# Feed-forward of a two-layer encoder step: the second hidden chunk with seven products in place of eight

## What is computed

```
def conv_ffn(x, conv_prev, w_up, conv_w, conv_b, w_down):
    u = x @ w_up
    ...
    c = conv_b
    for j in range(CONV_W):
        c = c + ue[:, j:j + T] * conv_w[j]
    a, b = jnp.split(c, 2, axis=-1)
    y = (jax.nn.silu(a) * b) @ w_down
    return y, ue[:, -(CONV_W - 1):]
```

## Time and profile before

| | us |
|---|---|
| median of 3 runs | 2957.55 (2957.21 to 2961.5) |
| the profiled execution, its own time | 2962.58 |
| its span, first to last instruction | 2960.7 |
| TensorE busy (95% of the span) | 2817.0 |
| VectorE busy (67%) | 1970.3 |
| ScalarE busy (37%) | 1098.0 |
| GpSimd busy (36%) | 1065.4 |

### The profile page before, as it was taken

The page is one execution under the profiler, slowest core; times in us unless marked ns, Lnnn a source line. Parts: engine busy times, 40 slices in busy tenths (PEclk is TensorE's granted clock), DMA queues, the critical chain, the costliest instruction groups (busy, mean ns, idle before and its releaser), DMA issues. The chain is left out here.

```text
span 2960.7 us, 47459 instructions
## 1 busy us (share of the span) xinstructions
PE 2817.0 (95%) x16927; PEld 2494.1 (84%) x16927; DVE 1970.3 (67%) x3414; ACT 1098.0 (37%) x2110; POOL 1065.4 (36%) x852
## 2 busy tenths in 40 slices
PE   8899799998999999999998898998999999999997
PEld 7455578886899999997887798997899999998886
DVE  3466654566578888888656464455468888888556
ACT  5334542333344333432113464334354333432112
POOL 1244421111236666662225101111136666662224
PEclk9999899999999999999999899999999999999999
DMA  3100350113212122124222111113212122124222
GB/s 116 51 8 13 121 186 22 37 40 111 86 65 81 66 74 81 66 91 175 91 91 94 54 37 42 30 45 114 83 67 81 66 74 81 66 91 175 91 91 102
DMA packets 90614, 233.61 MB, mean 79 GB/s; under 512 B 21514, under 2 KB 35995, under 8 KB 89428
## 3 DMA queue, kind: packets, MB, share of 16 engines
q1 hardware_dynamic: 90484, 231.85, 22.2%
HBM read 181.97 MB, written 50.50 MB: 79 GB/s over the span
## 5 line engine op out<-in xcount | busy, mean ns | idle before, releaser
L135 PE MATMUL psum<-xT_hi,tk_w 128*128 128x320 f32 (+1 forms) x1536 | 453.6, 295 | 2.8 <-ACT tk_u L2531 2.8
L137 PE MATMUL psum<-xT_hi,tk_w 128*128 128x320 f32 (+1 forms) x1536 | 453.7, 295 | 0.0
L136 PE MATMUL psum<-xT_lo,tk_w 128*128 128x320 f32 (+1 forms) x1536 | 452.5, 295 | 0.0
L2267 POOL TENSOR_TENSOR tk_w<-tk_sums,tk_w 128x512 fp32r<-128x512 f32 x160 | 306.9, 1937 | 170.3 <-ACT tk_w L2551 170.3
L135 PEld LDWEIGHTS psum<-xT_hi,tk_w 128*128 128x128 f32 x1536 | 289.4, 188 | 3.1 <-issue 3.1
L136 PEld LDWEIGHTS psum<-xT_lo,tk_w 128*128 128x128 f32 x1536 | 289.6, 189 | 0.0
L137 PEld LDWEIGHTS psum<-xT_hi,tk_w 128*128 128x128 f32 x1536 | 288.9, 188 | 0.0
L135 PE MATMUL psum<-tk_t,tk_w 128*128 128x256 f32 x960 | 284.4, 296 | 2.9 <-POOL tk_w L2267 2.9
L137 PE MATMUL psum<-tk_t,tk_w 128*128 128x256 f32 x960 | 284.5, 296 | 0.0
L136 PE MATMUL psum<-tk_t,tk_w 128*128 128x256 f32 x960 | 283.8, 296 | 0.0
L2949 DVE TENSOR_TENSOR x_or_mix<-x_or_mix,psum 128x512 f32<-128x512 f32 x288 | 195.3, 686 | 130.0 <-PE psum L137 129.3
(11 more groups left out here) (454 smaller groups left out, 7071.8 us busy)
## 6 DMA issues: line engine op xcount, KB each, us to landing
tk_wraw<-in_w_up SPq DMA_DIRECT2D x88, 512.0 KB, 4.2
ates_between_projections<-tk_g SPq DMA_DIRECT2D x44, 576.0 KB, 2.8
tk_graw<-ates_between_projections SPq DMA_DIRECT2D x44, 576.0 KB, 6.3
tk_draw<-in_w_down SPq DMA_DIRECT2D x44, 512.0 KB, 5.4
x_between_sublayers<-x_or_mix SPq DMA_DIRECT2D x18, 512.0 KB, 2.6
tk_resid<-x_between_sublayers SPq DMA_DIRECT2D x18, 512.0 KB, 7.9
s_ckv<-in_c_ckv SPq DMA_DIRECT2D x8, 1024.0 KB, 6.5
retw_raw<-in_w_ret SPq DMA_DIRECT2D x32, 256.0 KB, 3.3
```

Source lines behind the costliest of these rows:

```text
L135: nc.tensor.matmul(out, a[0], b[0], start=first, stop=False)
L136: nc.tensor.matmul(out, a[0], b[1], start=False, stop=False)
L137: return nc.tensor.matmul(out, a[1], b[0], start=False, stop=last)
L2267: nc.gpsimd.tensor_tensor(W7[:, i, 1], src, W7[:, i, 0].bitcast(F), ALU.subtract).then_inc(wl, 1)
```

## The change

Chunk 1 takes seven products too: `STD` goes from 2 to 1, the loops over seven-product chunks run one turn more (LOOP from 18 to 19), and `ORDER1`, `BANK1` and chunk 1's standard steps go. Now chunk 1 is the chunk in which T1 to T4 are used first. On DVE the four sums of weights stand ahead of the sums of x; the low halves of T2 and T3 stand right behind the sums of x, with chunk 0's convolution cut in two around T4's, and chunk 0's gate, which used to stand ahead of all of them, goes behind T1's. `t2_front` moves to the place of the gate's output, since `tk_sums` now holds its own place at that time. Of the raw weights chunk 2's go into `wraw` once chunk 1's A22 is split.

```
-    t2 = (m.at(tag + "t2_front", 90112, [P, 3, 576]), m.at(tag + "t2_end", 78848, [P, 1, 576]))
+    t2 = (m.at(tag + "t2_front", 9376, [P, 3, 576]), m.at(tag + "t2_end", 78848, [P, 1, 576]))
...
-    STD = 2
+    STD = 1
...
 (SP)
-            sp.wait_ge(us, 4)
-            raw(2)
             store_g(0)
-            store_g(1)
-            next_raw(2)
+            next_raw(1)
             with sp.Fori(0, LOOP) as r:
-                next_raw(r + 3)
-                store_g(r + 2)
+                next_raw(r + 2)
+                store_g(r + 1)
...
 (POOL)
-            split_up(1, 1)
+            for i in (A11, A12):
+                w_lo(1, i)
             keep_state(0, 1)
-            split_up(1, 0)
             keep_state(0, 0)
+            for i in (S2, S3):
+                w_lo(1, i)
             halos(1)
+            for i in (A22, S1, S4):
+                w_lo(1, i)
...
 (PE, in products)
-                        pe.wait_ge(tl, max(i - 1, 2))
+                        pe.wait_ge(tl, i - 1)
...
-                            pe.wait_ge(ur, min(13 + q, 16))
+                            pe.wait_ge(ur, (3, 4, 7, 8, 8, 8, 8)[q])
+                            if q == 4:
+                                pe.wait_ge(xf, NT)
...
 (PE)
-            for p, (ab, g) in enumerate(ORDER1):
...
-                up_part(ab, g, BANK1[p])
-            products(2, True)
+            products(1, True)
...
 (ACT)
+            w_hi(1, S2)
+            w_hi(1, S3)
             act.wait_ge(cl, 32)
             centre_tap(0, 1)
             centre_tap(0, 0)
-            take(1, 0)
-            take(1, 1)
+            t2_hi()
+            t3_hi()
+            act.wait_ge(tl, 1)
+            keep_s1(1, 0)
+            keep_s1(1, 1)
+            t4_hi()
+            act.wait_ge(um, 8)
+            nc.scalar.activation(T1x[0], t1[:], ACT.Copy).then_inc(th, 1)
             silu(0)
...
+            for i in (A22, S1, S4):
+                w_hi(1, i)
...
 (DVE)
+            for n in range(4):
+                w_sum(1, n)
             dve.wait_ge(xf, NT)
             sums(t1, x12, x11)
...
-            for ab in (1, 0):
-                conv(0, ab, 1)
-                conv(0, ab, 0)
+            t2_lo()
+            t_lo(1, T3x, t3[:])
+            for tap in (1, 0):
+                conv(0, 1, tap)
+            t_lo(2, T4x, t4[:])
+            for tap in (1, 0):
+                conv(0, 0, tap)
+            dve.wait_ge(cvd, 2)
+            take_11(1, 0)
+            take_11(1, 1)
+            t_lo(3, T1x, t1[:])
+            take_u2(1, 0)
+            take_u2(1, 1)
             gate(0)
...
```

More of the change, by code:

```diff
@@ L2253, in keep_state @@
                 if isinstance(j, int) and j < STD:
-                    pool.wait_ge(ur, (6, 8)[1 - ab] if j == 0 else (12, 16)[1 - ab])
+                    pool.wait_ge(ur, (6, 8)[1 - ab])
                 else:
@@ L2286, in _ @@
             keep_state(1, 1)
+            for i in (S2, S3, A22, S1, S4):
+                w_lo(2, i)
             keep_state(1, 0)
[L2288 to L2298, removed]
             with pool.Fori(0, LOOP) as r:
-                j = r + 3
+                j = r + 2
                 halos(j)
@@ L2545, in w_hi @@
                 if isinstance(j, int) and j == STD:
-                    act.wait_ge(um, 12 if i in (A11, A12) else 16)
+                    act.wait_ge(um, 6 if i in (A11, A12) else 8)
                     if i >= 4:
@@ L2554, in centre_tap @@
                 if isinstance(j, int) and j < STD:
-                    act.wait_ge(ur, (6, 8)[1 - ab] if j == 0 else (12, 16)[1 - ab])
+                    act.wait_ge(ur, (6, 8)[1 - ab])
                 else:
@@ L2637, in _ @@
                 if p == 5:
-                    hi_up(1, 1, 6)
-            hi_up(1, 0, 8)
+                    w_hi(1, A11)
+                    w_hi(1, A12)
+            w_hi(1, S2)
+            w_hi(1, S3)
             act.wait_ge(cl, 32)
@@ L2653, in _ @@
             centre_tap(1, 1)
-            for p in range(4, 8):
-                take(1, p)
+            for i in (S2, S3, A22, S1, S4):
+                w_hi(2, i)
             centre_tap(1, 0)
[L2657 to L2670, removed]
-                w_hi(3, i)
-            centre_tap(2, 0)
             def window(j):
@@ L2772, in sums, with w_sum @@
                 tlink(nc.vector.tensor_tensor(out[:, at, 512:576], a(1, ks), b(1, ks), ALU.subtract))
+            def w_sum(j, n):
+                jj = j - STD
+                a11, a12, a21, a22 = (wraw[:, ab, h * 512:h * 512 + 512] for ab in range(2) for h in range(2))
+                if n == 0:
+                    dve.wait_ge(la, 16 * j + 16)
+                    dve.wait_ge(lb, 16 * j + 16)
+                    ge(dve, wl, 7 * jj)
+                if n in (1, 3):
+                    dve.wait_ge(sd, 4 * jj + n)
+                x, y, op = ((a21, a22, ALU.add), (Sw[:, 0, :], a11, ALU.subtract), (a11, a21, ALU.subtract), (a12, Sw[:, 1, :], ALU.subtract))[n]
+                nc.vector.tensor_tensor(Sw[:, n, :], x, y, op).then_inc(sd, 1)
             def of_x(g, kh):
@@ L2908, in window_end @@
                 gate(j)
-            for ab in (1, 0):
-                conv(0, ab, 1)
-                conv(0, ab, 0)
-            gate(0)
-            t_lo(0, T3x, t3[:])
-            t2_lo()
-            t_lo(2, T4x, t4[:])
-            dve.wait_ge(tl, 2)
+            t2_lo()
[11 more added lines that the diff above has]
+            take_u2(1, 1)
+            gate(0)
+            take_u3(1, 0)
+            take_u3(1, 1)
+            take_21(1, 0)
+            take_21(1, 1)
+            take_p5(1)
             for n in range(4):
                 w_sum(2, n)
-            for ab in (1, 0):
-                conv(1, ab, 1)
-                conv(1, ab, 0)
-            gate(1)
-            t_lo(3, T1x, t1[:])
-            window(2, False)
-            take_p5(2)
-            for n in range(4):
-                w_sum(3, n)
-            window_end(2)
+            window_end(1)
             with dve.Fori(0, LOOP) as r:
-                window(r + 3)
-                take_p5(r + 3)
-                window_end(r + 3)
+                window(r + 2)
+                take_p5(r + 2)
+                window_end(r + 2)
             def d_lo(p, q):
```

34 lines of the change are left out of this document (7 added, 27 removed).

## The result

| | us |
|---|---|
| before, median of 4 runs beside it | 2957.82 (2957.21 to 2961.5) |
| after, median of 4 runs | 2986.04 (2982.2 to 2988.67) |
| ratio | 1.0093, 95% interval 1.0078 to 1.0108 |
| the profiled execution after, its span | 2984.4 |

The change makes the kernel slower by 28.2 us (by the interval 23 to 32). It was predicted at 2985, +27.3.

A forecast was written before the change was run, and what follows sets the result against it. PE, busy 95% of the span, was taken to bound the kernel, with DVE's chain making A22 late: +10.4 and +12.3 us for the layers plus 2 x 2.3 clock, +27.3 on 2957.55, so 2985 us, range 2967 to 2998.

The forecast's parts named there:

- its own chain: DVE's steps from the sums of weights to T1's low half, then A22's split: fifth product at 893.1 in layer 0.
- The raw weights: Layer 0, ahead of DVE's sums of weights: issued at 846.0, landed 5.9 us later at 851.9, a new wait.
- The sums of x: DVE, behind the sums of weights: 12.2 us undisturbed plus 5.1 us for POOL's four splits, ending at 871.9.
- the two ends given: Bounds on what POOL's four splits cost DVE within the sums of x: nothing, and 8.7 us.
- Rival 1: POOL's splits and DVE's sums run side by side, fifth product 5.1 us sooner per layer: +17.1, 2975 us; chance 0.17.
- T2, T3, T4, T1: DVE's low halves, 2.55 us each, convolution steps and takes between: T2's ends at 876.7, T1's at 890.9.
- PE's first wait: Chunk 1, ahead of the third product, until T2's low half is ready: 7.5 us in layer 0.
- From T1's low half to the fifth product: ACT rounds A22 and POOL splits it: 2.15 us, by the earlier row, so PE starts at 893.1.
- The clock: Slow clock on PE behind the long waits: 2.3 us lost in each layer, ends 1.6 and 3.05.
- the second wait: PE ahead of chunk 1's fifth product, from 883.1 to 893.1 in layer 0, until A22 is split.
- Chunk 2's raw weights: Asked for once A22 is split, landing before 900 against chunk 2's start at 902.7: covered by some 1 us.
- Rival 2: Everything is hidden: PE finds A22 at 875.5 and never waits, -11.4 us, 2946 us; chance 0.05.

The follow-up runs named there:

- e4: e3 with chunk 2's raw weights asked for on SP ahead of the store of chunk 0's gated values; 2977.71 us.
- e2: The change with chunk 0's convolution moved out of the A22 chain: first half ahead of T2's low half, second behind T1's; 2981.24 us.
- e3: The change with T1's halves made ahead of T2's, so A22, S1 and S4 need not wait; 2983.57 us.
- e1: The change with chunk 1's sums of weights behind the sums of x, and ACT's high halves of S2 and S3 behind T2's; 2977.29 us.
- e5: The change with the sums of weights ahead of the last x tile, where DVE idles, their transfer ahead of the last store of x; 2977.99 us.
- v2: The change with sums of weights and six tiles' sums of x early, T1's low half ahead of T4's, chunk 2's raw weights ahead of the store; 2961.02 us.
- v3: v2 with the order fitted to PE's requests: half of chunk 0's convolution ahead of T2's low half, S2 and A22 rounded sooner; 2956.21 us.

## Why the prediction was right

By its own chain, layer 0:

- **The raw weights** landed for DVE at 851.9, as forecast: the sums of weights start at 851.89.
- **The sums of x** took 870.58 - 854.56 = 16.0 us, where 17.3 were forecast. The four prolonged rows above (856.88, 858.42, 864.38, 866.09, which take 0.43, 2.29, 0.69 and 0.23 undisturbed) lost 3.8 us to POOL, not 5.1. This is the term that was mis-sized; it lay between the two ends given. Rival 1, that POOL takes nothing, falls.
- **T2, T3, T4, T1** run with the lengths of before, 1.2 to 1.4 us sooner than forecast. PE's first wait is 6.68 and 6.19 us (forecast 7.5).
- **From T1's low half to the fifth product** 892.60 - 889.49 = 3.11 us, where 2.15 were forecast, because the gate now stands beside the split of A22. That the two errors nearly cancel, 892.60 against 893.1, is luck. From chunk 1's start it is 30.18 us in layer 0 and 29.68 in layer 1, forecast 30.3 and 29.2. In layer 1 the first sum of weights starts 11.0 us ahead of chunk 1, not 12.0 as forecast; the other terms are as in layer 0.
- **The clock** took some 2 us behind the second wait of each layer (2.3 forecast; 0.50 until about 896.5, 4 us after the start).
- **Chunk 2's raw weights** are hidden behind the products, as forecast; e4 shows that DVE's sums from them aren't always.

What the prediction left open is what the wait hangs on. It summed one chain, from DVE's first row to A22, and for the change as written that chain is the longest. Read as a cause it would have misled: e2 and e3 shorten it by 4 and 7.7 us, and at most 1.4 us of that reach chunk 3. What counts is all the work and rest of DVE from the last x tile to chunk 2's takes, which e1, e4, e5 and v2 cut: by their expectations 4.1 us of it in e5 and some 13 in v2, and the stretch is 3.9 and 3.6 us shorter in e5, 11.7 and 12.8 in v2. The slow clock behind each wait adds to that, and no experiment changed it by itself. Rival 2, all hidden, fails for the reason that was given against it (what it has in its favour is misread: the earlier trace rows show DVE busy for 67% of the span, at rest for 33%); v2 and v3 remove most of that reason, and then PE still waits 3 to 5 us and the clock takes its share.

Not tried: taking work off DVE altogether (a step of the convolution, say). Each kernel here only moves DVE's work or its rests.

## What to carry to other kernels

When a change asks for an operand 25 us sooner, add up everything that its maker has to do until then, its rests too, and not only the chain to the operand: the order on the maker decides which consumer waits, the sum decides, for the most part, when the next stage starts. Measure a change on the stretch that it touches, from one fixed instruction to another; here differences of 3 to 4 us came out alike in both layers (e1, e5), where the times of one kernel's runs lay 4 to 15 us apart. An experiment that shortens one wait has shown something only if the next stage starts sooner.

## What was not expected of the hardware

**Small copies on POOL can be as dear as what DVE does beside them.** A copy of two columns, 0.19 us by itself, took 2.25 us in the change, and in v3 a copy of two columns and one of 16 between the splits of S2 and S3 took 5 us, each until a DVE instruction of 2.55 us was over; the split of S3 behind them took 3.57:

```profile
860.22 1.44 POOL L2262 TENSOR_TENSOR tk_w<-tk_sums,tk_w 128x512 fp32r<-128x512 f32 x1 [5.13 <-ACT tk_w L2537]
861.62 2.51 POOL L2253 COPY tk_new<-tk_u 128x2 f32<-128x2 f32 x1
864.07 2.54 POOL L2254 COPY tk_new<-tk_u 128x16 f32<-128x16 f32 x1
866.57 3.57 POOL L2262 TENSOR_TENSOR tk_w<-tk_sums,tk_w 128x512 fp32r<-128x512 f32 x1
```

```profile
860.43 3.65 DVE L2817 TENSOR_TENSOR tk_t<-tk_t_sum,tk_t 128x2304 fp32r<-128x2304 f32 x1
864.00 2.55 DVE L2817 TENSOR_TENSOR xT_lo<-tk_t,xT_hi 128x2304 fp32r<-128x2304 f32 x1
866.47 2.55 DVE L2817 TENSOR_TENSOR tk_t<-tk_t_sum,tk_t 128x2304 fp32r<-128x2304 f32 x1
```

In these rows the two engines take turns. The first copy ends at 864.13 and the second at 866.61, where the DVE rows end at 864.08 and 866.55; S3, rounded on ACT by 863.1, is split only by 870.1. In the other direction DVE's row at 860.43 took 3.65 us in place of 2.55, since the split of S2 ran until 861.66. The Trainium skill (SBUF — State Buffer, Who interferes with whom) has the rule, whoever is second blocks for the first one's whole length; the trace agrees. Neither engine's row shows it as idle time before the instruction: it is in the duration.

**The same waits don't always bring the slow clock.** In v2 PE waits 1.13, 1.77 and 2.36 us in layer 0, and 1.33, 1.77 and 2.36 in layer 1, with the same work between. Windows of PE behind the last of them, layer 0, then layer 1 (the granted clock, behind the brackets, is 0.53 and 1.00):

```profile
883.00:886.00 3.00, 3.00 (x15) 0.53 0.00 0
...
2215.00:2218.00 3.00, 3.00 (x23) 1.00 0.04 14
```

The stretch is 1.3 us longer in layer 0 for it. In the kernel before one wait of 2.20 us had a slow clock behind it. Why the two layers of v2 differ is not shown.
